# Differential attention: the last 512 of 1280 columns of each combination on POOL, the last copy of turned probabilities on DVE

## The reference

```python
s = jnp.einsum('bqhcd,bkhcd->bhcqk', q, k).astype(F32) * scale
p = jax.nn.softmax(s, axis=-1)
a = p[:, :, 0] - lam * p[:, :, 1]
return jnp.einsum('bhqk,bkhd->bqhd', a, v.astype(F32))
```

## Time and profile before

| | us |
|---|---|
| median of 3 runs | 2436.0 |
| lowest and highest | 2428.62, 2436.24 |
| the profiled execution, its own time | 2436.36 |
| its span | 2434.5 |
| `attend_pair`, first pair of the first layer | from about 585 to 686 |
| maxima on DVE (line 2164) in all | 196.7 busy, 144 of them |
| combines on DVE (line 2184) | 102.6 busy, 72 |
| exponentials on ACT (line 2117) | 177.4 busy, 144 |
| scores on PE (line 2049) | 126.1 busy, 400 |
| turns on PE (line 2066) | 104.7 busy, 656 |

### The profile page before, as it was taken

The page is one execution under the profiler, slowest core; times in us unless marked ns, Lnnn a source line. Parts: engine busy times, 40 slices in busy tenths (PEclk is TensorE's granted clock), DMA queues, the critical chain, the costliest instruction groups (busy, mean ns, idle before and its releaser), DMA issues. The chain is left out here.

```text
span 2434.5 us, 37576 instructions
## 1 busy us (share of the span) xinstructions
PE 1991.5 (82%) x14664; PEld 1644.5 (68%) x14664; DVE 1354.4 (56%) x2539; ACT 991.0 (41%) x2056; POOL 499.9 (21%) x646
## 2 busy tenths in 40 slices
PE   4698798897767778898976987989987677788988
PEld 2587677786555657787854877878775565577767
DVE  2336527858878367322744256158488783573256
ACT  5233333334858436411225333232338684353111
POOL 1312315411010100322224214135120100002212
PEclk7899898898989889999997999989898898899999
DMA  9760250141000310313336720520330003202231
GB/s 366 231 183 19 61 165 19 40 108 28 1 1 1 117 57 1 87 52 114 120 132 239 215 70 21 144 79 3 98 76 1 1 1 106 67 1 70 69 121 52
DMA packets 68607, 203.26 MB, mean 83 GB/s; under 512 B 7856, under 2 KB 11216, under 8 KB 64720
## 3 DMA queue, kind: packets, MB, share of 16 engines
q0 software_dynamic: 38016, 93.34, 13.8%
q1 hardware_dynamic: 25232, 98.08, 11.3%
q10 hardware_dynamic: 5184, 9.44, 1.0%
HBM read 180.83 MB, written 19.92 MB: 82 GB/s over the span
## 5 line engine op out<-in xcount | busy, mean ns | idle before, releaser
L590 PE MATMUL ps<-ring_lo,h_hi 128*128 128x512 f32 (+3 forms) x800 | 269.2, 336 | 0.0
L590 PE MATMUL ps<-h_hi,ring_lo 128*128 128x512 f32 (+1 forms) x688 | 251.2, 365 | 0.0
L2164 DVE TENSOR_REDUCE a_st<-ps 128x1 f32<-128x1280 f32 (+1 forms) x144 | 196.7, 1368 | 44.3 <-PE ps L2049 44.1
L2117 ACT ACTIVATE ring<-ps,a_st 128x1280 f32<-128x1280 f32 (+1 forms) x144 | 177.4, 1232 | 55.8 <-DVE a_st L2164 55.5
L2049 PE MATMUL ps<-a_k,a_q 128*128 128x512 f32 (+1 forms) x400 | 126.1, 426 | 54.4 <-ACT ring L2117 50.0
L590 PEld LDWEIGHTS ps<-ring_lo,h_hi 128*128 128x128 f32 x800 | 156.6, 196 | 13.4 <-issue 1.0
L590 PE MATMUL ps<-h_hi,g_proj_wh 128*128 128x512 f32 (+1 forms) x400 | 149.1, 373 | 12.6 <-DVE ring_lo L560 7.7
L590 PE MATMUL ps<-g_proj_xl,g_proj_wh 128*128 128x512 f32 (+1 forms) x400 | 148.5, 371 | 0.0
L590 PEld LDWEIGHTS ps<-h_hi,ring_lo 128*128 128x128 f32 x688 | 130.4, 190 | 21.4
L2066 PE MATMUL ps<-cst,ring 128*128 128x128 f32 x656 | 104.7, 291 | 43.9 <-ACT ring L2126 18.4
L2049 PEld LDWEIGHTS ps<-a_k,a_q 128*128 128x128 f32 x400 | 73.4, 211 | 83.7 <-ACT ring L2117 67.1
(11 more groups left out here) (359 smaller groups left out, 5278.9 us busy)
## 6 DMA issues: line engine op xcount, KB each, us to landing
ring<-in_w SPq DMA_DIRECT2D x16, 2048.0 KB, 7.5
b_proj_xl<-h_low POOLq DMA_DIRECT2D x32, 640.0 KB, 4.3
a_proj_xl<-h_low POOLq DMA_DIRECT2D x64, 320.0 KB, 3.2
ring<-in_w SPq DMA_DIRECT2D x24, 512.0 KB, 3.7
b_proj_xl<-h_low POOLq DMA_DIRECT2D x32, 320.0 KB, 4.2
c_proj_xl<-h_low POOLq DMA_DIRECT2D x32, 320.0 KB, 3.2
d_proj_xl<-h_low POOLq DMA_DIRECT2D x32, 320.0 KB, 3.2
h_low<-h_low SPq DMA_DIRECT2D x32, 256.0 KB, 2.0
```

The lines of the kernel that those rows point to most:

```text
L590: last = pe.matmul(out, left, right, start=k == 0 and j == 0, stop=k == KT - 1 and j == 2)
L2117: act.activation(p(u, c, n), ps[:, 3 * c:3 * c + 3, :].rearrange("p b n -> p (b n)")[:, 0:n], ACT.Exp, bias=st[:, 0:1], accum_out=st[:, 1: ...
L2164: dve.tensor_reduce(stat[:, u % SLOTS, c, 0:1], ps[:, 3 * c:3 * c + 3, :].rearrange("p b n -> p (b n)")[:, 0:n], AX.X, ALU.max, negate=Tru ...
```

## The change

The combine on DVE stops at column 768 for wide units. POOL, in a program of its own for this stage, does the other 512 columns in two instructions for each wide unit: it multiplies them of map 1 by the factor in place, waits for that, and adds them to map 0. PE waits for POOL ahead of the second chunk of turns (blocks 4 to 7, columns 512 to 1023), and ACT waits for it before it writes the buffer of map 1 again. Semaphore `scaled` counts products, `comb_last` sums.

The third chunk of turned probabilities (two blocks, 256 columns, from bank 6) is copied by DVE (`keep_last`) and not by ACT, behind the combine in DVE's order: in turn u, combine of u-1 and then the copy of u-2, which waits for PE's third chunk of that unit. The one semaphore for copies becomes two, `act_kept` and `dve_kept`, and the waits on it are split accordingly. DVE's loop runs two turns longer for it. Narrow units are done as before.

```diff
+    LAST = slice(6 * P, NT * P)
...
                 for n, (a, b) in enumerate(chunks(t)):
                     if n == 0:
-                        pe.wait_ge(t_kept.sem, before(u))
+                        pe.wait_ge(act_kept.sem, on_act(u))
+                        pe.wait_ge(dve_kept.sem, on_dve(u))
+                    if n == 1 and wide(u):
+                        pe.wait_ge(comb_last.sem, on_dve(u + 1))
...
                     if n == 2:
-                        pe.wait_ge(t_kept.sem, before(u) + 1)
+                        pe.wait_ge(act_kept.sem, on_act(u) + 1)
...
-                pe.wait_ge(t_kept.sem, before(u + 2))
-                if u + 2 < NU:
-                    pe.wait_ge(t_kept.sem, before(u + 2) + min(2, len(chunks(units[u + 2][0]))))
+                pe.wait_ge(dve_kept.sem, on_dve(u + 2))
+                pe.wait_ge(act_kept.sem, on_act(min(u + 3, NU)))
...
                 if c == 1 and u >= 2:
                     act.wait_ge(comb.sem, u - 1)
+                    act.wait_ge(comb_last.sem, on_dve(u - 1))
...
-                for n, (a, b) in enumerate(chunks(t)):
+                for n, (a, b) in enumerate(chunks(t)[0:2]):
...
                 dve.wait_ge(factored.sem, u + 1)
-                n = keys(t) * P
+                n = LAST.start if wide(u) else keys(t) * P
...
+            def keep_last(u):
+                if wide(u):
+                    a, b = chunks(units[u][0])[2]
+                    dve.wait_ge(t_mm.sem, before(u) + 3)
+                    if u >= 4:
+                        dve.wait_ge(o_mm.sem, u // 2 - 1)
+                    dve.tensor_copy(aT[u % 4][:, a:b, :], ps[:, 6, 0:(b - a) * P].rearrange("p (k t) -> p k t", t=P)).then_inc(dve_kept.sem, 1)
...
+            for u in range(NU + 2):
+                if u < NU:
+                    maximum(u, 0)
+                if 1 <= u <= NU:
+                    inverses(u - 1)
+                    factor(u - 1)
+                if u < NU:
+                    maximum(u, 1)
+                if 1 <= u <= NU:
+                    combine(u - 1)
+                if u >= 2:
+                    keep_last(u - 2)
+            dve.wait_ge(dve_kept.sem, on_dve(NU))
+
+        @block.gpsimd
+        def _(pool):
             for u in range(NU):
...
+                if wide(u):
+                    a, b = p(u, 0, T)[:, LAST], p(u, 1, T)[:, LAST]
+                    pool.wait_ge(factored.sem, u + 1)
+                    pool.tensor_tensor(b, b, stat[:, u % SLOTS, 0, 3:4].broadcast_to([P, LAST.stop - LAST.start]), ALU.mult)\
+                        .then_inc(scaled.sem, 1)
+                    pool.wait_ge(scaled.sem, on_dve(u + 1))
+                    pool.tensor_tensor(a, a, b, ALU.add).then_inc(comb_last.sem, 1)
+            pool.wait_ge(comb_last.sem, on_dve(NU))
```

More of the change, by code:

```diff
@@ L2002, in attend_pair @@
     name = f"a{pair}"
-    (s_mm, mx, exped, inverse, factored, comb, t_mm, t_kept, o_mm, o_kept, back_mm, o_done, dv, lam_a) = (
-        signal(f"{name}_{n}") for n in ("scores", "max", "exp", "inverse", "factor", "combined", "turns", "turn_kept", "out_mm", "out_kept",
+    (s_mm, mx, exped, inverse, factored, comb, scaled, comb_last, t_mm, act_kept, dve_kept, o_mm, o_kept, back_mm, o_done, dv, lam_a) = (
+        signal(f"{name}_{n}") for n in ("scores", "max", "exp", "inverse", "factor", "combined", "scaled_last", "combined_last", "turns", "turn_kept_act", "turn_kept_dve", "out_mm", "out_kept",
                                         "back", "out_scaled", "dve", "lam"))
@@ L2026, in before, with wide, on_dve, on_act @@
         return sum(len(chunks(units[i][0])) for i in range(u))
+    def wide(u):
+        return len(chunks(units[u][0])) > 2
+    def on_dve(u):
+        return sum(wide(i) for i in range(u))
+    def on_act(u):
+        return before(u) - on_dve(u)
+    LAST = slice(6 * P, NT * P)
     with ExitStack() as own, nc.Block() as block:
@@ L2088, in back @@
                 pe.wait_ge(o_kept.sem, i + 1)
-                if u < NU:
-                    pe.wait_ge(t_kept.sem, before(u) + min(2, len(chunks(units[u][0]))))
+                pe.wait_ge(act_kept.sem, on_act(min(u + 1, NU)))
                 pe.transpose(ps[:, 7, P:2 * P], oT[:, :], C(env, "ident")).then_inc(back_mm.sem, 1)
@@ L2126, in keep @@
                     act.activation(aT[u % 4][:, a:b, :], ps[:, 6 + n % 2, 0:(b - a) * P].rearrange("p (k t) -> p k t", t=P),
-                                   ACT.Copy).then_inc(t_kept.sem, 1)
+                                   ACT.Copy).then_inc(act_kept.sem, 1)
             def keep_out(i):
@@ L2193, in _ @@
                 dv.link(dve, dve.tensor_tensor(nlam[:, :], nlam[:, :], W(env, "lam_init")[:, 0:1], ALU.subtract))
-            for u in range(NU):
[L2195 to L2206, removed]
+            for u in range(NU + 2):
[13 more added lines that the diff above has]
+        def _(pool):
+            for u in range(NU):
+                if wide(u):
[6 more added lines that the diff above has]
+            pool.wait_ge(comb_last.sem, on_dve(NU))
 def stage_window_attention(nc, env):
```

## The result

The changed kernel takes **2459.1 us**, the median of six runs (2446.19 to 2460.89), against 2437.6 for the kernel before in six runs (2428.62 to 2441.05). The ratio is 1.008, with a 95% interval of 1.0053 to 1.0108: slower by 0.8%. The forecast of 2431 with its range of 2424 to 2442 missed on the wrong side. The profiled execution took 2460.38 (span 2458.6, granted clock 0.915 against 0.920 before).

A forecast was written before the change was run, and what follows sets the result against it. The bound was taken as a chain across engines, 10.52 us per two units. 21 periods x -0.13 = -2.7 and 4 starts x -0.55 = -2.2 made -4.9 us on 2436.4: 2431 by the median's footing, range 2424 to 2442.

The forecast's parts named there:

- (5): Attention, DVE's combine against POOL's SBUF instructions: next to no wait at the slack unit, 0.06 us lost on the chain.
- (1): DVE's combine in wide attention units shrinks from 1280 to 768 columns, saving 0.53 us.
- (2): DVE's copy of the last 128x256 chunk, directly behind the combine, costs 0.34 us; net -0.19 us for a unit.
- (3): ACT in attention loses the third copy, which is off the chain; nothing credited.
- (4): POOL's product and sum of 128x512 per unit take 1.26 + 0.08 + 1.30 = 2.64 us; as a wait, free.
- (6): Each attention stage's start saves 1.1 us, of which 0.55 is kept for meetings; at the end nothing lost or won.
- POOL in the way: At the attention combine, both POOL instructions run at 1.35 us or more and block DVE: 2445 us, chance 0.18.
- the harder form: POOL's sum gets in ahead of DVE's combine: 1.4 us at the slack unit, 1.25 hidden, more on the chain.
- The no-meeting case: In attention, POOL is done before the chain's combine arrives and isn't met in the start: 2427 us, chance 0.27.
- The rival by which ACT's copy counts: ACT's third copy is behind 0.25 us of idle ahead of PE's value product: 2422 us, chance 0.05.
- the one by which the maximum hides the gain: DVE's maximum behind the odd combine turns out bound by PE: 2436 us, as good as no change, chance 0.10.
- Other stages should not move at all: Stages outside the attention over pairs of heads keep their times: no change.

The follow-up runs named there:

- run 3: The changed kernel, with POOL's sum also waiting for DVE's combine of the same unit; 2433.4 us, ratio 0.9981 to the kernel before.
- run 2: The kernel before with only the shorter combine and POOL's two instructions, all three copies on ACT; 2423.2 us, ratio 0.9955.
- 4: The kernel before with the shorter combine and POOL's two instructions, the sum waiting for DVE's combine, all copies on ACT; 2423.1 us, ratio 0.9948.
- run 9: Kernel 4 with 768 columns on POOL and 512 on DVE in the chain's units; 2423.3 us, ratio 0.9918 to the kernel before.
- 1: The kernel before with the third copy on DVE, no POOL work and all 1280 columns combined on DVE; 2463.7 us, ratio 1.0121.
- run 8: The changed kernel with a POOL memset of 128x40 between product and sum; 2427.0 us, ratio 0.9958 to the kernel before.
- run 5: The kernel before plus a POOL product and sum of 128x512 per wide unit that nothing reads; 2450.8 us, ratio 1.006.
- run 7: The kernel before plus an unneeded DVE memset of 128x400 behind each wide combine on the chain; 2469.7 us, ratio 1.0141.
- run 6: The changed kernel measured once more without an edit; 2455.1 us, ratio 1.0073 to the kernel before.
- 10: Kernel 4 measured again without an edit; 2420.2 us, ratio 0.992 to the kernel before.
- 11: The kernel before plus four POOL memsets of 128x512 for each wide unit; 2435.6 us, ratio 0.9988.

## Why the prediction was wrong, step by step

The profiled execution was to lose 4.9 us and gained 24.1, 29 us apart. The middles of the stages were given -2.7 and made +3.0, the starts -2.2 and +4.5: these 12 us are step (5), and run 3, with the order set, doesn't have them (195.7 and 115.6 us against 198.9 and 118.6 before). The tails, given nothing, made +4.8, and the code outside the stages +11.9, of which 8.0 is one mLSTM stage and 3.9 scatter. Of these the traces show the clock as the form that the loss takes, not why it came.

**(1) The shorter combine: right.** Undisturbed it takes 1.01 (run 3), as forecast.

**(2) The copy on DVE: right in itself.** 0.33 from the copy's start to the next maximum (649.27 to 649.60), and the net of a chain unit, -0.19, is what run 3 shows (10.52 to 10.32). What the step left out is that the copy stands in the unit with slack as well. There it delays the next factor, and with it POOL, against a chain that doesn't move: the chain's combine loses 0.05 in run 2 and 0.39 with the copy.

**(3) ACT's third copy worth nothing: right as far as tried.** Putting it back on ACT costs nothing and saves DVE's 0.34 (3 against 4).

**(4) POOL's pair: mis-sized.** The product takes 1.04 instead of 1.26, since I took a sum of two full operands for a product with one repeated column; the hand-over and sum came as said (0.08, 1.28). The hint stood in rows 7: at 256 columns the product takes 0.61 and the sum 0.69. With that 0.08 doubled the product would have been at 1.14, an estimate, and the sum at factor + 1.51, ahead of the combine's 1.53. A quarter of the 4497 ns that the Trainium skill (GPSIMD Engine Reference, section 3.1) gives for 2048 columns was 1.12, an estimate: nearer to the product's 1.04, farther from the sum's 1.28. The trace doesn't contradict the page's figure but the quartering. The sums of 512 and 768 columns (1.28, 1.82 in run 9) make 2.11 ns for a column and 0.20 us that doesn't shrink, which puts 2048 columns at an estimated 4.5 us. That the wait for POOL is free was right (run 3).

**(5) The neighbour: here the prediction failed,** at "the combine slips in ahead of the sum". I had the combine's arrival right to a hundredth (factor + 1.53) and the sum's start at factor + 1.63 (1.55 and a gap of 0.08). It was factor + 1.42. With 0.10 us between two forecasts I made a certainty of the order, where the price of the other order was 0.97. The second half fell with it: the chain's combine was to come at factor + 2.87, from gaps "both taken as they were". But the 0.97 used DVE's idle time, the next factor came late against a maximum that didn't move with it, and the combine arrived at factor + 2.11 (658.65 - 656.54), deep in the sum, which ended at factor + 2.71: 0.39 lost instead of 0.06. With the order set, it arrives at factor + 2.92 (run 3). The period went +0.19 instead of -0.13, within my bounds for the pair (-0.19 to +0.29) but by another way.

With the terms as each trace shows them, the rule of the forecast, that a period moves by the net of the chain's unit alone, holds for every kernel but one. The table has the terms of the chain's unit, their sum on 10.52, and the period measured where the clock doesn't drop:

| kernel | combine | meeting | copy or memset | gives | measured |
|---|---|---|---|---|---|
| the change | -0.53 | +0.39 | +0.34 | 10.72 | 10.71 |
| 1, copy alone | 0 | 0 | +0.34 | 10.86 | 10.85 |
| 2, POOL alone | -0.53 | +0.05 | 0 | 10.04 | 10.04 |
| 3 and 8, POOL's sum second | -0.53 | 0 | +0.34 | 10.33 | 10.32 |
| 4, order, copies on ACT | -0.53 | 0 | 0 | 9.99 | 9.98 |
| 5, idle POOL pair | 0 | +0.24 | 0 | 10.76 | 10.77 |
| 7, memset with its gaps | 0 | 0 | +0.55 | 11.07 | 11.07 |
| 9, 512 columns left on DVE | -0.80 | 0 | 0 | 9.72 | 9.81 |

Only run 9 is off, by 0.09. The unit with slack enters through the time of the meeting: the more is put into it, the earlier the chain's combine comes behind its factor and the deeper in the sum (2.11 and 0.39 with the copy).

**(6) The ends.** The start was to save 0.55 a stage and lost 1.1 (+4.5 in four). In order, as in run 3, it saves 0.75 (118.6 to 115.6). The tails, to which I gave nothing, cost 4.8: in all four the granted clock is at its lower level for 3.4 us, 4 to 9 us behind the last maximum, instead of in one (14.2 us without the drop and 15.8 with it in the kernel before). It is the same in run 6, and in run 8, with 13.9 in all four tails, it isn't there at all; why it comes is not shown.

**The rivals.** The slower one, POOL in the way, is what happened, in the harder form that I named beside it, "if the sum gets in ahead of the combine". Its price there was too high at the slack unit, 1.4 us with 1.25 hidden, where 0.97 was lost and all of it hidden; the "more on the chain" to which I gave no number was 0.39. The condition of the main form was the wrong way round: POOL's instructions at 1.35 us or more. It took a **shorter** product for the sum to be first. The no-meeting case, to which the page's figure led, has the same mistake: a faster POOL was taken for a POOL that is less in the way. The rival by which ACT's copy counts is refuted (3 against 4; its 2422 was reckoned from the no-meeting case, from the forecast it would have been 2426), and the one by which the maximum hides the gain too (period 10.32 in run 3).

**"Other stages should not move at all"** was wrong by 8 us, and the clock is the only difference that the traces show. Between the second and third stage PE is at its lower level for 174 us, against 150 before. In it is one unbroken stretch of 44 us, most of it in the mLSTM stage above, whose instructions are unchanged. It stands in the change and in runs 1, 3, 6 and 8, all with the copy on DVE, and isn't there in 2, 4, 5, 7, 10 and 11. Run 9, without the copy, has two of 24 and 31 us there instead and 174 in all. Each of these is one execution, and those of 3 and 8 were 11 and 15 us above the medians of their kernels, so not every execution need have the stretch. Why a copy in one stage should set PE's clock in another, some 700 us later, no run here explains. **This stays open.** At a granted clock of 0.918 to 0.920 over the whole execution, the three of the change take 2446 to 2450, and the 25 of the kernel before in the three comparisons 2431 to 2443, with medians of 2434 to 2436. That is some 12 to 14 us, about what the attention stages grew by (12.2); it suggests, and doesn't show, that the rest of the 20 is the clock elsewhere.

## What to carry to other kernels

When work goes to POOL beside a DVE instruction with two SBUF inputs, first ask who starts first in each unit. Where two arrivals lie within some 0.2 us, don't forecast the order: set it with a wait, so that the engine on the chain goes first (here that was free, and worth some 24 us). Slack is not free either: work put into it (the copy) delays what that engine hands on, here the factor that starts POOL. Price it together with every meeting whose time it shifts.

## What the runs showed of the hardware that I had not expected

- A POOL product of 128x512 with one repeated column takes 1.04 us, a sum of two different tensors 1.28, a sum of one tensor with itself 1.04 (run 5). The second full operand costs 0.24.
- A blocked instruction is recorded as a long one, not as a wait: 1.98 for 1.01 on DVE, 2.08 for 1.28 on POOL. The idle time ahead of it shows nothing, so blocking has to be looked for in durations, least against median.
- A factor of 128x1 beside a POOL sum is stretched too (0.39 for 0.22, run 9).
- The time that DVE loses in a meeting with a sum is what is left of the sum less 0.2 us: 0.97 lost with 1.17 left (652.72 to 653.89), 0.39 with 0.60, 0.73 with 0.91 (run 2), 0.79 with 0.99 (run 5). In rows 9 it is less 0.13.
- A few tenths of a microsecond in each period can cost more than themselves. In run 7 the memset and the gaps around it add 0.55 to a period, some 12 us in 21, and the stages grew by 30, with 42 us more at the lower level.
